# Hybrid decoder trunk, two layers: eight groups of data per layer transposed by VectorE squares and a trip through device memory

## What is computed

```python
for l in range(DEPTH):                       # DEPTH = 2
    h = _rmsnorm(x, ln_g[l])
    u = h @ w_in[l]                          # 2048 x 6232
    y_a = gla(...)  * silu(g_a)              # gated linear attention, 4 heads
    y_b = ssd(...)                           # state-space mixer with its gate g_b and a norm, 512 wide
    y_c = mla(...)  * silu(g_c)              # causal attention, 4 heads of 128 + 64 rotated columns
    y_d = dilated_attention(...) * silu(g_d) # 4 heads of 128
    x = x + concat[y_a, y_b, y_c, y_d] @ w_out[l]
```

## Time and profile before

| | |
|---|---|
| median of 3 runs | 824.13 us (824.00 to 824.54) |
| the profiled execution, whole | 823.59 us |
| its span in the trace | 821.6 us |
| PE busy | 816.4 us (99%) |
| DVE busy | 625.2 us (76%) |
| ACT busy | 478.2 us (58%) |
| DMA queue of SP, share of 16 engines | 57.0% |

### The profile page before, as it was taken

How to read it: one execution, slowest core, us unless ns; L and a number is a source line. 1 busy time by engine, 2 the same in 40 slices (tenths; PEclk the granted TensorE clock), 3 DMA queues, 4 the chain that set the end, 5 groups by cost and what they waited for, 6 DMA issues and landing times.

```text
span 821.6 us, 11397 instructions
## 1 busy us (share of the span) xinstructions
PE 816.4 (99%) x4244; PEld 693.0 (84%) x4244; DVE 625.2 (76%) x1118; ACT 478.2 (58%) x788; POOL 54.1 (7%) x64
## 2 busy tenths in 40 slices
PE   9999999999999999999999999999999999999998
PEld 5888888999888888888888888889998888888886
DVE  6678799876886986678965977979769868965542
ACT  6665534777865566433556464357697665654341
POOL 7200000200200000000000000002012000000000
PEclk9999999999999999999999999999999999999999
DMA  9956634566654445655576655457657433456653
GB/s 333 352 204 211 192 129 153 145 208 180 208 176 154 129 132 201 191 191 187 177 253 184 200 161 169 129 147 200 191 173 220 164 129 129 158 177 210 196 189 119
DMA packets 47607, 150.98 MB, mean 184 GB/s; under 512 B 5504, under 2 KB 6192, under 8 KB 47552
## 3 DMA queue, kind: packets, MB, share of 16 engines
q1 hardware_dynamic: 47040, 149.98, 57.0%
q10 hardware_dynamic: 320, 0.21, 0.1%
q0 software_dynamic: 192, 0.07, 0.1%
HBM read 148.13 MB, written 2.11 MB: 183 GB/s over the span
## 4 chain that ended last, share of the span: by engine, by line
PE 91%; DVE 7%; issue 2%; DMA 1%; SPq 0%; ACT 0%; DVEq 0%
PE gemm L665 26%; PE gemm L674 26%; PE gemm L666 26%; DVE arena L1323 3%; DVE w_lo L1354 2%; PE pairs L857 1%; PE pairs L846 1%; PE pairs L833 1%; PE pairs L838 1%; PE pairs L834 1%; PE pairs L795 1%; PE pairs L731 1%; DVE arena L1433 1%; PE pairs L872 1%; DMA u<-in_xT_dram 1%
## 5 line engine op out<-in xcount | busy, mean ns | idle before, releaser
L1354 DVE TENSOR_TENSOR w_lo<-raw,w_hi 128x1024 fp32r<-128x1024 f32 (+2 forms) x295 | 324.7, 1110 | 144.4 <-ACT w_hi L997 142.9
L665 PE MATMUL gemm<-w_hi,a_hi 128*128 128x512 f32 (+1 forms) x1144 | 421.6, 374 | 0.0
L666 PE MATMUL gemm<-w_hi,a_lo 128*128 128x512 f32 (+1 forms) x1144 | 414.4, 368 | 0.0
L997 ACT ACTIVATE w_hi<-raw 128x1024 fp32r<-128x1024 f32 (+2 forms) x295 | 281.0, 967 | 191.4 <-PE gemm L674 136.1
L674 PE MATMUL gemm<-w_lo,a_hi 128*128 128x512 f32 (+1 forms) x1144 | 281.8, 368 | 0.3
L665 PEld LDWEIGHTS gemm<-w_hi,a_hi 128*128 128x128 f32 x1144 | 215.2, 188 | 35.6 <-issue 1.3
L666 PEld LDWEIGHTS gemm<-w_hi,a_lo 128*128 128x128 f32 x1144 | 215.3, 188 | 33.0
L674 PEld LDWEIGHTS gemm<-w_lo,a_hi 128*128 128x128 f32 x1144 | 203.2, 188 | 36.6 <-DVE w_lo L1354 2.0
L573 POOL TENSOR_TENSOR st<-st,powers 128x4 f32<-128x4 f32 (+2 forms) x8 | 8.6, 1074 | 431.5 <-ACT arena L1075 213.4
L1195 ACT ACTIVATE arena<-arena,st 128x128 f32<-128x128 f32 (+1 forms) x32 | 13.1, 444 | 35.4 <-DVE st L1616 35.4
L1027 ACT ACTIVATE u<-gemm,st 128x512 f32<-128x512 f32 (+1 forms) x40 | 22.1, 605 | 18.8 <-PE gemm L674 18.8
(11 more groups left out here) (200 smaller groups left out, 639.0 us busy)
## 6 DMA issues: line engine op xcount, KB each, us to landing
raw<-in_weights_dram SPq DMA_DIRECT2D x225, 512.0 KB, 4.1
raw<-in_weights_dram SPq DMA_DIRECT2D x64, 278.0 KB, 3.1
raw<-in_weights_dram SPq DMA_DIRECT2D x6, 384.0 KB, 3.4
x<-in_x_dram SPq DMA_DIRECT2D x4, 512.0 KB, 6.2
o<-ssd_rows SPq DMA_DIRECT2D x8, 256.0 KB, 4.9
param_rows<-in_params_dram SPq DMA_DIRECT2D x2, 904.0 KB, 7.1
u<-in_xT_dram SPq DMA_DIRECT2D x3, 512.0 KB, 8.1
out_dram<-x SPq DMA_DIRECT2D x3, 512.0 KB, 6.4
```

The costliest lines, as they stand in the source:

```text
L665: pe.matmul(acc_t[t], a_hi[:, k, tok[t]], hi, start=k == 0, stop=False)
L666: pe.matmul(acc_t[t], a_lo[:, k, tok[t]], hi, start=False, stop=False)
L997: A_(w_hi[:, g % SPLIT, 0:c], raw[:, g % RAW, 0:c], ACT.Copy).then_inc(hi_done, 1)
L1354: TT(w_lo[:, g % SPLIT, 0:c], raw[:, g % RAW, 0:c], w_hi[:, g % SPLIT, 0:c].bitcast(F32), ALU.subtract).then_inc(split_done, 1)
```

## The change

Eight blocks of a layer are now turned in three steps. DVE turns the 32 by 32 squares inside the four groups of 32 partitions (`turn_squares`, two instructions of 128 partitions by 512; `ssd_y_squares`, four of 128 by 256). SP stores the result to device memory (`squares_out`, 512 KB). SP fetches it back with the squares permuted over the partitions (`squares_back`, four DMAs of 128 KB, in runs of 1 KB). A reader then undoes the order of the columns in its access pattern. The blocks are mla q, mla k (without their rotated columns), dil q, dil k, the state-space sums, and the results 0, 1 and 2. The stages `ssd yb`, `mla qT`, `mla kT`, `dil qT`, `dil kT` and `yT 2` leave PE; `mla rT` and `yT 3` stay. `ssd y`'s copy leaves ACT, since `gated 1` reads the fetched block itself. The 16-instruction turns of the results 0 and 1 leave DVE.

```diff
-          "mla kv 1": KV_AT, "ssd Y": 76, "ssd yb": 81, "mla qT": 85, "mla kT": 86, "mla rT": 87, "mla S 0": 89, "mla PT 0": 92,
-          "mla S 1": 93, "mla O 0": 94, "dil qT": 95, "mla PT 1": 96, "dil kT": 97, "mla O 1": 98, "dil S 0": 99,
+          "mla kv 1": KV_AT, "ssd Y": 76, "mla rT": 87, "mla S 0": 89, "mla PT 0": 92,
+          "mla S 1": 93, "mla O 0": 94, "mla PT 1": 96, "mla O 1": 98, "dil S 0": 99,
...
-Y_TURN = {1: 97, 0: 101}
-Y_SPLIT = [110, 112, 113, 117]
+Y_TURN = {1: 97, 0: 100, 2: 107}
+Y_SPLIT = [110, 112, 114, 117]
...
+        for _j, _n in Y_TURN.items():
+            SQUARES[f"y {_j}"] = A(_j * 1024, 1024), A(_j * 1024, 1024), _n
+        SQUARES["ssd y"] = A(4096, 1024), A(4096, 1024), 81
+        SQUARES["mla q"] = fold[:, :], A(3072, 1024), 79
+        SQUARES["mla k"] = A(6656, 1024), u[:, 1, 0:1024], 83
+        SQUARES["dil q"] = fold[:, :], u[:, 0, 0:1024], 90
+        SQUARES["dil k"] = A(6656, 1024), u[:, 1, 0:1024], 92
+
+        HEADS_AT = {"mla q": 86, "mla k": 88, "dil q": 95, "dil k": 97}
...
+            def squares_out(l, name):
+
+                sp.wait_ge(*reached("dve", l)(f"{name} squares"))
+                sp.dma_start(squares_d[name], SQUARES[name][0]).then_inc(squares_out_done[name], 16)
+
+            def squares_back(l, name):
+
+                sp.wait_ge(squares_out_done[name], 16 * (l + 1))
+                away, to = squares_d[name].rearrange("(i b) (f c) -> f b i c", b=32, f=4), SQUARES[name][1]
+                for f in range(4):
+                    sp.dma_start(to[32 * f:32 * f + 32].rearrange("b (i c) -> b i c", i=4), away[f]).then_inc(squares_in[name], 16)
...
+                    for name, (_, _, at) in SQUARES.items():
+                        if n == at + 5:
+                            squares_out(l, name)
+                        if n == at + 7:
+                            squares_back(l, name)
...
                 def heads_T(name, dst):
-                    act_.wait_ge(*pe(name))
-                    A_(dst, pair_of(name).rearrange("p b (k s) -> p (b k) s", k=2), ACT.Copy).then_inc(*signal("act", name))
+
+                    act_.wait_ge(squares_in[name], 16 * 4 * (l + 1))
+                    act_.wait_ge(*dve("mla rope" if name[:3] == "mla" else "dil rope 1"))
+                    A_(dst.rearrange("p h (t i a) -> p i (h t) a", t=T, i=4), SQUARES[name][1].rearrange("p (i c a) -> p i c a", i=4, a=32), ACT.Copy).then_inc(*signal("act", name + "T"))
...
+            def turn_squares(to, rows):
+
+
+                to = to.rearrange("p (f k t a) -> p t k f a", f=4, k=4, t=T)
+                for t in range(T):
+                    last = v.transpose(to[:, t], rows[:, t].rearrange("p k (f b) -> p k f b", f=4))
+                return last
...
+                    v.wait_ge(*pe("mla S 1"))
+                    turn_squares(SQUARES[f"y {j}"][0], o[:, j].rearrange("p t (k c) -> p t k c", k=4)).then_inc(*sig(f"y {j} squares"))
...
+                    if (m, i) == ("mla", 0):
+                        v.wait_ge(*me(f"gated {GB}"))
...
-                    if n == 93:
+                    if n == 91:
                         gated(GB)
```

More of the change, by code:

```diff
@@ L230 @@
         "gla level 6, gla level 7, gla out, ssd cum, ssd gcol, ssd CB, ssd xs, "
-        "mla cT, ssd Y, ssd yb, mla qT, mla kT, mla rT, "
-        "mla S 0, mla PT 0, mla S 1, mla O 0, dil qT, mla PT 1, dil kT, mla O 1, dil S 0, dil PT 0, dil S 1, dil O 0, "
-        "dil PT 1, dil O 1, yT 2, yT 3",
+        "mla cT, ssd Y, mla rT, "
+        "mla S 0, mla PT 0, mla S 1, mla O 0, mla PT 1, mla O 1, dil S 0, dil PT 0, dil S 1, dil O 0, "
+        "dil PT 1, dil O 1, yT 3",
     "act":
@@ L238 @@
         "mla crs sum, ssd gcol, evac 6, ssd silu 0, ssd exp 0, evac 7, mla cT, ssd xD, ssd exp 1, mla q 0, mla q 1, mla rs 0 sum, "
-        "evac 8, mla kv 0, mla kv 1, mla rs 1 sum, dil rs 0 sum, evac 9, dil rs 1 sum, ssd y, mla qT, mla kT, evac 10, "
-        "mla rT, mla P 0, ssd rs sum, mla PT 0, mla P 1, evac 11, dil qT, mla PT 1, dil kT, dil P 0, dil PT 0, "
+        "evac 8, mla kv 0, mla kv 1, mla rs 1 sum, dil rs 0 sum, evac 9, dil rs 1 sum, mla qT, mla kT, evac 10, "
+        "mla rT, mla P 0, ssd rs sum, dil qT, mla PT 0, mla P 1, dil kT, evac 11, mla PT 1, dil P 0, dil PT 0, "
         "evac 12, dil P 1, dil PT 1, yT 0, yT 1, yT 2, evac 13, yT 3",
@@ L247 @@
         "conv 0 3, conv 0 4, conv 0 5, ssd CB, mla cn, ssd E 0, ssd xdt, mla cT, ssd E 1, ssd M 0, ssd M 1, "
-        "mla n 0 0, mla n 0 1, ssd yT, mla n 1 0, mla n 1 1, mla rope products, mla rope, dil n 0 0, dil n 0 1, "
-        "dil n 1 0, dil n 1 1, dil rope 0 products, dil rope 0, dil rope 1 products, dil rope 1, mla max 0, "
[2 rows of a table removed]
+        "mla n 0 0, mla n 0 1, ssd yT, mla q squares, mla n 1 0, ssd y squares, mla n 1 1, mla k squares, mla rope products, mla rope, dil n 0 0, dil n 0 1, "
+        "dil n 1 0, dil n 1 1, dil rope 0 products, dil rope 0, dil q squares, dil rope 1 products, dil rope 1, gated 1, dil k squares, mla max 0, "
[2 rows of a table added]
         "yT 2, y 3, yT 3, x turn 0, x turn 1, x turn 2",
@@ L796, in ssd_Y @@
                     last.then_inc(*signal("pe", "ssd Y"))
-                def ssd_yb():
-                    pe.wait_ge(*dve("ssd yT"))
-                    ps = bank()
-                    for f in range(SSD_DI // P):
-                        for t in range(T):
-                            last = pe.transpose(ps[:, t, f * P:(f + 1) * P], ssd_yT(f)[:, t * P:(t + 1) * P], ident)
-                    last.then_inc(*signal("pe", "ssd yb"))
                 def mla_cT():
@@ L1275, in _ @@
                         head_sums("dil", 1)
[L1276 to L1287 removed]
+                    for name, to in (("mla q", mqT), ("mla k", mkT), ("dil q", dqT), ("dil k", dkT)):
+                        if n == HEADS_AT[name]:
+                            heads_T(name, to)
+                    if n == slot("mla rT"):
+                        mla_rT()
                     for m in ("mla", "dil"):
@@ L1551, in ssd_add, with ssd_y_squares @@
                     TT(bsq, bsq, pair_of("ssd Y"), ALU.add).then_inc(*sig("ssd yT"))
+                def ssd_y_squares():
+                    v.wait_ge(*me("ssd yT"))
+                    to = SQUARES["ssd y"][0].rearrange("p (i t k b) -> p k t i b", i=4, t=T, k=4)
+                    for f in range(SSD_DI // P):
+                        last = v.transpose(to[:, f], ssd_yT(f).rearrange("p (t i a) -> p t i a", t=T, i=4))
+                    last.then_inc(*sig("ssd y squares"))
                 def ssd_norm():
@@ L1728, in _ @@
                             head_norm("mla", 1, t)
+                    for name in HEADS_AT:
+                        if n == SQUARES[name][2]:
+                            head_squares(name)
+                    if n == SQUARES["ssd y"][2]:
+                        ssd_y_squares()
                     if n == 83:
```

93 lines of the change are left out of this document (49 added, 44 removed), and 4 rows, old and new, of the table ORDER.

## The result

| | before | changed |
|---|---|---|
| median | 824.13 us (5 runs, 824.00 to 825.47) | 832.64 us (5 runs, 829.51 to 835.50) |
| profiled execution, span | 823.59, 821.6 us | 835.5, 833.7 us |
| PE busy | 816.4 us (99%) | 811.2 us (97%) |
| DVE, ACT busy | 625.2, 478.2 us | 615.1, 476.3 us |

A forecast was written before the change was run, and what follows sets the result against it. PE, busy 99% of the span, was taken as the bound. Of 5.45 us a layer off PE, waits left 1.6 net, 3.2 us in all: 820.9 us, range 815.5 to 827.

The forecast's parts named there:

- What leaves PE: Six batches of eight transposes a layer leave PE, 0.91 us each: 5.45 us a layer, 10.9 us gross.
- What comes onto DVE: Squares ahead of the first maxima make them 5.4 us later; PE then waits some 3.4 us before PT 0.
- The trip of mla k: Store and fetches of mla k land at 238, between 235.4 and 242.7; hidden behind DVE's lateness up to 238.7.
- From there each microsecond costs one a layer: Each microsecond that mla k lands after 238.7 makes a layer one microsecond longer.
- the trip comes late: Rival: mla k lands late and S 0 waits for `mla rT`; slower from about 241, 829 at 242.7; chance 0.11.
- The clock: Rival: PE's waits drop its clock to 1.2 GHz, up to 2.72 us per unit; one a layer makes 826; chance 0.05.
- Squares twice as long: Rival: squares of 128x512 on DVE take 0.87 us, giving 823.5; chance 0.23, shared with a trip a little late.
- serial squares: Rival: DVE turns the four partition groups one after another, squares of 2.8 us, near 855 us; chance 0.02.
- the clean gain: Rival: the whole gain stays, 813.2 us; kept in greater part, 813 to 818, chance 0.12.
- O 0 without a wait: ACT's copies for O 0 end at 265.3 and PE comes at 265.8: no wait, by 0.5 us.
- O 1 at 0.2: PE waits about 0.2 us before O 1, for ACT's copy of PT 1, done at 279.1.
- the three signs of being wrong: DVE idle between slots 84 and 92; the copy of mla k finding its data ready; granted clock under 1.

The follow-up runs named there:

- e2: Kernel before, with results 0, 1 and 2 alone by squares and trip; queries, keys and state-space sums stay on PE: 822.17 us, ratio 0.9977.
- e3: Changed kernel with mla q, mla k and the state-space sums turned on PE as before; dil q, dil k and results by squares: 818.39 us, ratio 0.9933.
- e10: e8 with ACT's copies of dil q and dil k one place later each: 816.34 us, ratio 0.9909.
- e5: Changed kernel with 20 products nobody reads on PE, filling its wait ahead of unit 89: 830.47 us.
- e12: The kernel of e5 again, beside the changed kernel on the same chip: 832.59 us, ratio 1.0104.
- e13: Changed kernel with all trips issued, but ACT's copies of mla q and mla k read DVE's squares in place and DVE doesn't wait for the landing: 823.43 us.
- e6: Changed kernel with the state-space sums and mla q turned on PE again, mla k the only early trip: 823.43 us, ratio 0.9988.
- e7: Changed kernel with mla k alone turned on PE again: 821.17 us, ratio 0.9968.
- e8: Changed kernel with mla q and mla k turned on PE again: 818.41 us, ratio 0.9936.
- e14: Changed kernel with the state-space sums alone turned on PE again: 820.61 us, ratio 0.9966.
- e15: Changed kernel with the stores of mla q, ssd y and mla k issued earlier, from ACT instead of SP: 833.47 us, ratio 1.0113.
- e4: Changed kernel with ACT's copy of mla k moved from slot 88 to 90, behind the evacuation: 825.23 us, ratio 1.0020.
- e11: The changed kernel once more, unaltered, which gave the second trace (832.33 us): median 831.56 us, ratio 1.0094.

## Why the prediction was wrong

**What leaves PE** was right. 0.91 us a batch: e2, e3 and e10 gave back 2, 6 and 8 of them in full. The exchange itself pays where its trips are covered.

**What comes onto DVE** was over-sized a little. The groups of DVE's instructions after the change (busy us, mean ns | idle before):

```profile
L1350 DVE STREAM_TRANSPOSE arena<-u 128x512 f32<-128x512 f32 x8 | 5.2, 685 | 0.0
L1590 DVE STREAM_TRANSPOSE arena<-u 128x256 f32<-128x256 f32 x8 | 2.8, 412 | 0.0
```

Two squares of 128x512 take 1.30 us, 0.65 each, where I took 0.71; four of 128x256 take 1.42, where I took 4 x 0.44 = 1.77. P 0 starts at 254.06 without trips, against 255.4, and PE waits 1.85 us and not 3.4. Without trips the kernel takes 817.15 us, 3.7 under the forecast, which had them hidden; 2 x (3.4 - 1.85) = 3.1 of it is this term.

**The trip of mla k** is the step that failed, in its size: the term that the prediction called the one on which the sum leans. From issue at 230.1 (230.4 measured) I took 3.5 us for the store, 1.3 for issues and 3 for the last fetch, landing at 238. Measured: 7.7, 1.3 and 4.8, landing at 244.3, behind even my upper bound of 242.7. The store took 7.7 and 9.9 us here and 6.5 and 6.6 in the second trace, all above the bound of 6.4 from the earlier trace rows; the landing there, 243.2, is behind the bound too. (With the filling of e5 and e12 it took 5.9 to 8.8 us, and e5's first landing, 241.5, lies inside it.) From the landing on the next step held: S 0 follows by 7.9 us (7.75 forecast). "From there each microsecond costs one a layer" gives (244.3 - 238.7) x 2 = 11.2 us on 820.9, 832.1, where 832.6 came; but that is luck. The base without waits for trips is 817.15 and not 820.9, the landing is the first layer's of the slowest execution, 3.7 us of that execution are waits at O 0 and O 1, and e13 shows that 6.3 us of loss stay when nobody reads the landing. Late landing and late weights act in the same wait and don't add up.

The cause of the wrong size is in the argument against the rival: "a load of 512 KB lands in 4.1 us under that traffic". That was the traffic before, and the median over the whole span. The stretch was at 61.5% of 16 engines, had the average of 57%, and three trips move 3.1 MB more (beside nine loads between 215 and 240, where I wrote seven). At the 13 points a megabyte that 4.74 MB in 61.5% give, this is an estimate of 41 points, and the sum is 102%. By e6, e7, e8 and e14, which added 13.6 to 18.5 points a megabyte, it is low. I counted issues and durations, and never added up the demand. That the full queue is what made the transfers slow is shown by taking trips away (e14) and by issuing earlier without gain (e15); how its time divides between bytes and the form of the fetches is not shown.

**The rival "the trip comes late"** had the right place and the right slope, and 0.11 was far too small a chance. **The clock** rival, 0.05, saw its event (0.54 of full clock over the 3 us behind the wait), but not its price in the changed kernel: ACT's chain, not PE, decides in that stretch. In e4 and e13 it has one, 1.4 to 2.5 us in a layer whose S 0 waited 3.7 to 3.8 us, near the 2.72 that the rival wrote. The rule of the Trainium skill cited there (TensorE: Matmul & The Clock Gate, Part 1) agrees with the rows: half the clock behind 4.93 and 3.73 us of idle array. **Squares twice as long**, **serial squares** and **the clean gain** fell. **O 0 without a wait**, by 0.5 us, and O 1 at 0.2: measured up to 1.5, since the copies of dil q and dil k, late by their fetches, stand ahead of those of PT on ACT; in e10 they stand behind, and the waits are gone. Two of the three signs of being wrong came: DVE stood idle 4.87 us between slots 84 and 92, and the clock fell.

Open: the changed kernel's spread (829.5 to 835.5, against 0.5 us for e10). Four traces have all its trips, two of them with the filling. The store of mla k takes 6.0 and 6.7 us in the two layers of e5 (829.9 us), 6.5 and 6.6 in e11 (832.3), 8.8 and 5.9 in e12 (833.9), 7.7 and 9.9 in the profiled execution (835.5): their sums stand in the order of the times. What makes one store slower than another was not tried.

## What to carry over

Before data are sent over device memory, take the DMA engines' share in that very stretch, not over the span, and add the megabytes of all new transfers at the share that a megabyte has there. That estimate is low where the new transfers move fewer bytes in an engine's time, as the fetches did here. At 90% and more, in this case, no duration of the old trace held, and the stream that was there before (the weights) came late as well; spread the trips, or take fewer. A wait on a late landing costs more the more stands behind its reader: put the reader behind the work that doesn't need it, as e4 and e10 did. And ask what PE waits for right behind an idle stretch: if another engine's chain decides, the low clock is hidden, as in the changed kernel; if PE's own work does, it is paid, as in e4 and e13.

## What I had not expected of the hardware

Squares of 256 elements are shorter on 128 partitions than on 32: 412 against 436 ns, and four in a row 1.42 us against 1.74 (64 of them took 27.9). A full DMA queue moved 215 GB/s with the fetches in runs of 1 KB in flight, where stores and weights alone moved 420 (e14). And 4.93 us without a product took TensorE's clock to 1.2 GHz with no measurable loss (831.56 us with it, 832.59 without), since the engine that decided there was another; 3.73 us without one, right ahead of S 0, cost 2.5 us.
